# Column order of the moving tile and of PSUM in the first layer's up projection of a two-block kernel

## What is computed

```python
def conv_ffn(h, w_up, dw_w, dw_b, w_down):
    u = dwconv(h @ w_up, dw_w, dw_b)        # w_up 1024 x 5632, width-3 convolution along the tokens
    a, g = jnp.split(u, 2, axis=-1)
    return (a * jax.nn.silu(g)) @ w_down    # w_down 2816 x 1024
```

## Time and profile before

| what | value |
|---|---|
| median of three runs | 2155.14 us (2152.23 to 2159.14) |
| span of the profiled execution, first to last instruction | 2160.2 us |
| TensorE busy | 2103.9 us, 97% |
| VectorE busy | 1659.1 us, 77% |
| ScalarE busy | 1050.5 us, 49% |
| TensorE's granted clock, mean | 0.995 of full |
| the stretch of the eight slots that the change touches | 1250.77 to 1424.85 us of the span |

### The profile page before, as it was taken

How to read it: one execution, slowest core, us unless ns; L and a number is a source line. 1 busy time by engine, 2 the same in 40 slices (tenths; PEclk the granted TensorE clock), 3 DMA queues, 4 the chain that set the end, 5 groups by cost and what they waited for, 6 DMA issues and landing times.

```text
span 2160.2 us, 34277 instructions
## 1 busy us (share of the span) xinstructions
PE 2103.9 (97%) x14202; PEld 1861.1 (86%) x14202; DVE 1659.1 (77%) x2986; ACT 1050.5 (49%) x1714; POOL 109.7 (5%) x86
## 2 busy tenths in 40 slices
PE   5999999999999999999999999999999999999999
PEld 4988889989878878788888888888989789999999
DVE  5988979888598777567874889884469777776984
ACT  3457635665333554542223555451354547545673
POOL 0000000000000321300000000000000313000000
PEclk9999999999999999999999999999999999999999
DMA  9884578545331211135552455545352212664554
GB/s 343 275 267 151 191 231 246 176 145 169 98 78 59 63 55 40 40 118 166 185 174 98 139 194 195 194 138 202 112 139 97 79 59 79 195 215 157 181 182 127
DMA packets 282092, 326.72 MB, mean 151 GB/s; under 512 B 28752, under 2 KB 261712, under 8 KB 281808
## 3 DMA queue, kind: packets, MB, share of 16 engines
q1 hardware_dynamic: 280656, 322.43, 46.3%
q10 hardware_dynamic: 1280, 2.10, 0.3%
HBM read 321.36 MB, written 1.05 MB: 149 GB/s over the span
## 4 chain that ended last, share of the span: by engine, by line
PE 84%; DVE 13%; ACT 1%; DMA 1%; issue 0%; SPq 0%; DVEq 0%; ACTq 0%
PE ps L800 83%; DVE parts L2270 2%; DVE ring L2223 1%; DVE arena L2363 1%; DVE arena L2704 1%; DVE parts L2672 1%; PE ps L1351 1%; DMA ring<-w_in 1%; DVE parts L2486 0%; DVE arena L2883 0%; DMA ring<-w_ada_t 0%; ACT hT L1826 0%; DVE arena L2360 0%; DVE arena L2833 0%; ACT w_high L1616 0%
## 5 line engine op out<-in xcount | busy, mean ns | idle before, releaser
L800 PE MATMUL ps<-parts,w_high 128*128 128x256 f32 (+1 forms) x6776 | 1143.9, 320 | 3.3 <-DVE parts L3022 0.9
L800 PEld LDWEIGHTS ps<-parts,w_high 128*128 128x128 f32 x6776 | 983.2, 189 | 111.7 <-issue 11.4
L800 PE MATMUL ps<-parts,parts 128*128 128x256 f32 (+1 forms) x3772 | 650.9, 314 | 10.6 <-DVE parts L2270 4.3
L800 PEld LDWEIGHTS ps<-parts,parts 128*128 128x128 f32 x3772 | 546.7, 189 | 61.9 <-DVE parts L2270 5.5
L1616 ACT ACTIVATE w_high<-ring 128x1024 fp32r<-128x1024 f32 (+2 forms) x452 | 450.8, 1013 | 229.9 <-PE ps L800 145.1
L2672 DVE TENSOR_TENSOR parts<-ring,w_high 128x1024 fp32r<-128x1024 f32 (+2 forms) x292 | 334.2, 1151 | 110.2 <-ACT w_high L1616 110.1
L2223 DVE CUSTOM_DVE_ANT_0 ring<-ring,c_rows,cols 128x1024 f32<-128x1024 f32 x144 | 182.9, 1279 | 26.4 <-DMA ring<-ada_w_t 12.0
L2169 POOL TENSOR_TENSOR parts<-ring,w_high 128x512 fp32r<-128x512 f32 x80 | 109.3, 1391 | 1724.2 <-ACT w_high L1616 1724.2
L2704 DVE SCALAR_TENSOR_TENSOR arena<-arena,cols 128x512 f32<-128x512 f32 (+1 forms) x240 | 159.5, 664 | 6.3
L800 PE MATMUL ps<-arena 128*128 128x257 f32 (+6 forms) x800 | 138.7, 391 | 3.2 <-DVE arena L2812 2.7
L800 PEld LDWEIGHTS ps<-arena 128*128 128x128 f32 (+2 forms) x800 | 94.6, 167 | 35.4 <-issue 13.5
(11 more groups left out here) (274 smaller groups left out, 1726.7 us busy)
## 6 DMA issues: line engine op xcount, KB each, us to landing
ring<-w_in SPq DMA_DIRECT2D x118, 1024.0 KB, 5.3
ring<-ada_w_t SPq DMA_DIRECT2D x48, 1024.0 KB, 4.9
ring<-ffn_w_up SPq DMA_DIRECT2D x44, 1024.0 KB, 5.3
ring<-w_ada_t SPq DMA_DIRECT2D x24, 1024.0 KB, 8.3
ring<-w_out SPq DMA_DIRECT2D x16, 1024.0 KB, 5.2
ring<-ffn_w_down SPq DMA_DIRECT2D x16, 1024.0 KB, 5.3
ring<-w_out SPq DMA_DIRECT2D x16, 512.0 KB, 4.6
ring<-w_mlstm_out SPq DMA_DIRECT2D x8, 1024.0 KB, 5.3
```

The lines of the kernel that those rows point to most:

```text
L800: return tensor.matmul(o, a, b, start=first, stop=last)
```

## The change

A table gives a column order for slots 3 to 10. In those slots of the first layer (`lo` is 0 there) the output bank, the high activation tile and the low activation tile of each matmul are viewed as a x b x c columns and walked with a and b exchanged: c columns in a row are taken from each of the a equal parts of the 512 columns in turn. Output and moving tile are walked in the same order, so each result still lands in its own column. Weights, sums, waits and the number of instructions are as before. In slots 0 to 2, in the last layer and in every other product the order stays straight.

```diff
+def column_order(pattern, **sizes):
+
+    def ordered(x):
+
+        return x.rearrange(pattern, **sizes)
+
+    return ordered
+
+
+COLUMN_ORDERS = {3: column_order("p (a b c) -> p b a c", a=2, c=2), 4: column_order("p (a b c) -> p b a c", a=2, c=16),
+                 5: column_order("p (a b c) -> p b a c", a=2, c=8), 6: column_order("p (a b c) -> p b a c", a=2, c=32),
+                 7: column_order("p (a b c) -> p b a c", a=4, c=16), 8: column_order("p (a b c) -> p b a c", a=2, c=64),
+                 9: column_order("p (a b c) -> p b a c", a=8, c=4), 10: column_order("p (a b c) -> p b a c", a=2, c=4)}
...
-            def split_strip(o, name, j, lo, low=None, k0=0, first=True, last=True, end=TT, high=None, parts=None, ahead_of_lows=None, ahead_of_last=None, late=0):
-
+            def split_strip(o, name, j, lo, low=None, k0=0, first=True, last=True, end=TT, high=None, parts=None, ahead_of_lows=None, ahead_of_last=None, late=0, order=None):
+
+                order = order or (lambda x: x)
+                o = order(o)
...
-                    return high_parts_of(*phase)[:, k0 + k, lo:end] if high is None else high[k][:, lo:end]
+                    return order(high_parts_of(*phase)[:, k0 + k, lo:end] if high is None else high[k][:, lo:end])
...
-                        mm(o, half_high(n)[:, k, :], low[:, k0 + k, lo:end], False, False)
+                        mm(o, half_high(n)[:, k, :], order(low[:, k0 + k, lo:end]), False, False)
...
-                            project_slot(part, s, lo)
+                            for j in range(2):
+                                project_strip(part, 2 * s + j, lo, order=None if lo else COLUMN_ORDERS.get(s))
```

More of the change, by code:

```diff
@@ L847, in split_strip @@
                     pe.wait_ge(*when(("h_low",) + parts + (k0 + k,)))
-                    i = mm(o, half_high(n)[:, k, :], low[:, k0 + k, lo:end], False, last and k == nk - 1)
+                    i = mm(o, half_high(n)[:, k, :], order(low[:, k0 + k, lo:end]), False, last and k == nk - 1)
                 return i
```

## The result

The changed kernel takes 2177.89 us (median of four runs, 2176.83 to 2179.07) against 2154.51 us before: 23.4 us or 1.0098 times as long, with a 95% interval of 1.0084 to 1.0113. It is slower by more than the 0.3% that can be told from no change.

What follows compares the result with a forecast made beforehand. The prediction took TensorE's matmul stream to bound the kernel in slots 3 to 10. All terms were 0, summing to 0 us on the 2155.1 us median, so it forecast 2155.1 us, range 2145 to 2182 us.

Steps and rivals of the forecast that it cites:

- What bounds the kernel: Slots 3 to 10: TensorE is always busy and waits for nobody; a nanosecond per changed matmul adds 768 ns.
- Other engines at 0: Instructions, waits, DMAs and other engines stay as before, ScalarE's copy out of the bank included: cost 0.
- The write into PSUM at 0: Writing the output bank in pieces in slots 3 to 10 costs 0, set beside the read without a row.
- the sentence of the Trainium skill on PSUM: Non-contiguous PSUM access significantly slows matmuls; backed two cycles per column, +155.9 us in all slots; several slots, chance 0.15.
- The value that I take is 0, for reading and writing alike: Slots 3 to 10: reading the moving tile and writing PSUM in pieces both add 0 us.
- the float32 passes with one jump: Query rotation at L1307, moving tile in two pieces of 256 columns: 429.3 ns a pass against 429.7 straight.
- the milder rival: Slots 3 to 10: shorter runs bring the extra cycle per 16 columns earlier, +17.9 us; within a shared chance of 0.18.
- the rival of a gain: Slots 3 to 10: the 32 extra cycles per matmul go away, 9.1 us faster, 2146.0 us; chance 0.06.
- A jump costs a cycle: Slots 3 to 10: each of 63,744 jumps loses one cycle, +26.6 us, 2181.7 us; within a shared chance of 0.18.
- The milder form: Pieces of 16 or more stay at 32 extra cycles, shorter ones pay more: +17.9 us, 2173.0 us; shared chance 0.18.
- Two cycles per column in slot 3 alone: Slot 3's 96 matmuls fall to two cycles per column, +19.5 us, 2174.6 us; within a shared chance of 0.18.
- The rate taken as the upper bound, 429.7 ns: Slowest 512-column stream seen, straight float32 passes; if every changed matmul fell to it, +155.9 us.

Runs made afterwards that it cites:

- about four times the dose: The changed kernel with pieces of 2 columns (a=2, c=2) in all of slots 3 to 10: 2243.87 us, ratio 1.0422 to the kernel before.
- the map: The changed kernel with another a and c in each of 28 strips from slot 2, first slot's float32 matmuls in pairs: 2201.72 us, one run.

## Why the prediction was wrong

**What bounds the kernel: right.** TensorE alone sets these slots, and a nanosecond per matmul is a nanosecond at the end. Stretch (+22.35 us) and time (+23.4 us) agree, and so they do at about four times the dose.

**Other engines at 0: right.** **The write into PSUM at 0: right as a number, by luck.** The kernel that only writes in order shows the 0 now. But the prediction had no row for it and took it over from the read, whose own value was wrong. Keeping the sentence of the Trainium skill on PSUM (the section named above) as a rival with a chance of its own was sound; it fell.

**The step that failed: "The value that I take is 0, for reading and writing alike", for the reading.** It measured +22.35 us. I took it from the row nearest in kind, the float32 passes with one jump. Those were the wrong rows to read a price from, for two reasons that the prediction itself named and then set aside. They have one jump in 512 columns. And they run at two cycles per column, so a line of four columns is wanted every 8 cycles, though straight fp32r gets one every 4.25 (544 / 128); even pieces of 2 lose only 5% there. The right row stood in the text: 544 cycles for 512 columns. As the read of one column shows (215.8 ns), the straight read was already what set the rate, so that more work for the read had nothing to hide behind. I called the cause of the extra cycles unknown, which it was then, and gave it no weight beyond the milder rival and the rival of a gain.

**The rivals.** "A jump costs a cycle" gave +17.9 to +26.6 us, and the result lies between. Its mechanism is still wrong: eight jumps of 64 cost nothing, and a shift of 8 bytes doubles the price of the same jumps. The milder form has slots 4, 6 and 7 at 5.44 us a strip; they take 5.76, 5.68 and 5.55. It was the price of this rival, not an understanding of the read, that set the upper end of the range, 2182 us. So that the range holds the 2177.89 us is luck. "Two cycles per column in slot 3 alone" had the dearest slot right, but not its size, +10.9 us where +19.5 was worked out, nor the whole, as most of the other slots pay too; and it is the read that pays. The rate taken as the upper bound, 429.7 ns as the slowest seen, was no bound: in the map pairs with a of 4 or more take 431 to 487 ns. The extra cycles did not go away in any of the orders.

**What the sum should have been.** By lines alone only slot 3 pays, 256 lines in place of 128: 453 ns a matmul, +21.7 us. That this is near the 22.35 us is chance: slot 3, with its two streams, paid only half of it, 10.9 us. The other 11.5 us come from pieces that fill whole lines, 4 to 32 columns long, at 2 to 23% over straight. Both departures are measured but not explained. The price of the whole-line pieces does not follow the number of jumps, the distance, tried with two streams, moves it by a few per cent at most, it changes with the number of parts in no simple order, and it is all but gone at 64. It stays open.

No order was faster than straight, so there is no version here that beats the kernel before.

## What to carry to other kernels

When a stream runs at a rate a little off its engine's clock, as 544 cycles for 512 columns here, ask what sets that rate before adding to it, and don't take a price from rows that run at half the speed. For fp32r matmuls in this kernel, let the moving tile be read in runs of 64 columns or more, and let shorter ones start and end on 16 bytes (they still cost up to 23%); never in pairs. The order in which a matmul writes its PSUM bank is free down to pairs, so where a result has to be reordered, do it on the write.

## What the runs showed of the hardware

- The straight fp32r read is what holds a 512-column matmul at 226.67 ns; the same matmul with one column read 512 times takes 215.8 ns. Straight reads of 504 columns, from column 0, 2 or 4, take 226.67 ns as well.
- Where the lines limit the read, a line of 16 bytes costs about 1.771 ns: 128 lines take 226.67 ns, 256 lines 453 (pieces of 2, a=16; with other a of 4 or more 431 to 487), and a shift of 8 bytes takes pieces of 4 from 222.2 to 466.7 ns (a=4). Aligned pieces of 4 to 32 columns cost up to 23% above their lines, and pieces of 2 in two streams 25% less (340 ns).
- The Trainium skill (Advanced Engine Details and Errata, section Memory Cachelines) has lines of 16 bytes in SBUF, and the runs agree. It asks for at least two hits on a line; two are not enough here for full performance: pairs, with two hits, take 431 to 487 ns with a of 4 or more.
- Writing PSUM in pieces of two columns, at every a from 2 to 128, leaves fp32r matmuls at 226.67 ns; plain float32 matmuls that write single columns stay at 215.8 ns.
- Within a strip the price of a pattern is steady to a nanosecond (340 ns in slot 3), swings in a short cycle (246 and 254 ns in turn in slot 10) or swings without one (228 to 277 ns for pieces of 8 with a=8 in the map). From kernel to kernel it can differ: 340.0 and 333.3 ns for the same pairs.
